# A hybrid attention block: second norm by token halves, stacked low-rank and gate products, modulation sums inside a product tile

## What is computed

```python
mod = silu(c) @ ada_w + ada_b                      # six vectors of 1024
h = rmsnorm(x, norm1_w) * (1 + scale1) + shift1
gq, gk, gv, gr, g_lr, aq, ak, av, ma, mb = split(h @ w_in)     # g_lr has 16 columns
log_a = log_sigmoid(g_lr @ gate_w2 + gate_b) / 16  # [512, 512]
o_gla = rmsnorm(gla_chunked(gq, gk, gv, log_a)) * silu(gr)
y_attn = dilated_attention(aq, ak, av) @ w_attn    # rotary, three groups, 12 heads
x = x + gate1 * ((sigmoid(ma) * (o_gla @ w_gla) + sigmoid(mb) * y_attn) @ w_out)
h2 = rmsnorm(x, norm2_w) * (1 + scale2) + shift2
x = x + gate2 * (conv_ffn_hidden(h2, w_up) @ w_down)           # d_ff 2816
out = rmsnorm(x, final_w)
```

## Time and profile before

| | |
|---|---|
| median of 3 runs | 977.91 us (975.19 to 981.04) |
| the profiled execution as a run | 976.27 us |
| its span, first to last instruction | 974.5 us |
| PE busy | 929.3 us, 95% |
| DVE, ACT, POOL busy | 522.8, 373.1, 95.8 us |
| mean granted clock of PE | 0.969 of 2.4 GHz |
| DMA | 112.68 MB, 116 GB/s mean |

### The profile page before, as it was taken

The page is one execution under the profiler, slowest core; times in us unless marked ns, Lnnn a source line. Parts: engine busy times, 40 slices in busy tenths (PEclk is TensorE's granted clock), DMA queues, the critical chain, the costliest instruction groups (busy, mean ns, idle before and its releaser), DMA issues.

```text
span 974.5 us, 11999 instructions
## 1 busy us (share of the span) xinstructions
PE 929.3 (95%) x4659; PEld 780.5 (80%) x4659; DVE 522.8 (54%) x643; ACT 373.1 (38%) x457; POOL 95.8 (10%) x66
## 2 busy tenths in 40 slices
PE   2689999999999999999999997999999999999996
PEld 2589887779988888888888885888888888888885
DVE  4994775654765546563244436645554556533223
ACT  5362113457543524635222323433433343332225
POOL 4720433000000000000002222000000000000003
PEclk9589999979999999999999998999999999999998
DMA  9925764605253121212232533143334332322302
GB/s 320 362 90 181 212 194 128 212 27 173 91 170 87 44 75 57 87 44 87 86 121 84 184 88 86 49 117 93 86 87 116 99 86 86 125 91 86 123 6 87
DMA packets 114015, 112.68 MB, mean 116 GB/s; under 512 B 4516, under 2 KB 104230, under 8 KB 111671
## 3 DMA queue, kind: packets, MB, share of 16 engines
q1 hardware_dynamic: 113255, 109.96, 35.9%
q10 hardware_dynamic: 720, 2.16, 0.6%
HBM read 104.77 MB, written 4.19 MB: 112 GB/s over the span
## 4 chain that ended last, share of the span: by engine, by line
PE 87%; DVE 6%; DMA 2%; issue 1%; POOL 1%; ACT 1%; SPq 1%; DVEq 0%; POOLq 0%; ACTq 0%
PE bank L1486 25%; PE bank L1488 25%; PE bank L1487 25%; DVE ada_in L959 2%; PE bank L1695 2%; POOL rope L534 1%; PE bank L1877 1%; DMA ada_in<-in_ada_w_dram 1%; PE bank L1641 1%; PE bank L1716 1%; PE bank L1682 1%; PE bank L1578 1%; DVE w_lo L993 1%; DVE h_lo L1414 1%; DMA raw<-in_w_in_dram 1%
## 5 line engine op out<-in xcount | busy, mean ns | idle before, releaser
L1486 PE MATMUL bank<-h_hi,w_hi 128*128 128x512 f32 (+1 forms) x696 | 276.7, 398 | 0.4 <-DVE w_lo L993 0.4
L1488 PE MATMUL bank<-h_hi,w_lo 128*128 128x512 f32 (+1 forms) x696 | 272.4, 391 | 0.0
L1487 PE MATMUL bank<-h_lo,w_hi 128*128 128x512 f32 (+1 forms) x696 | 272.1, 391 | 0.0
L1486 PEld LDWEIGHTS bank<-h_hi,w_hi 128*128 128x128 f32 (+1 forms) x696 | 130.5, 188 | 29.0 <-issue 1.9
L1488 PEld LDWEIGHTS bank<-h_hi,w_lo 128*128 128x128 f32 (+1 forms) x696 | 130.3, 187 | 29.0 <-issue 0.8
L1487 PEld LDWEIGHTS bank<-h_lo,w_hi 128*128 128x128 f32 (+1 forms) x696 | 130.5, 187 | 27.9 <-issue 1.1
L1000 DVE TENSOR_TENSOR w_lo<-raw,w_hi 128x2048 fp32r<-128x2048 f32 x32 | 73.4, 2293 | 88.8 <-ACT w_hi L574 88.8
L993 DVE TENSOR_TENSOR w_lo<-raw,w_hi 128x2048 fp32r<-128x2048 f32 (+3 forms) x48 | 88.2, 1848 | 58.3 <-ACT w_hi L566 58.3
L1440 DVE SCALAR_TENSOR_TENSOR conv<-bank,vecs,conv 128x511 f32<-128x511 f32 x88 | 65.7, 748 | 67.4 <-ACT conv L888 61.9
L566 ACT ACTIVATE w_hi<-raw 128x2048 fp32r<-128x2048 f32 (+2 forms) x45 | 73.4, 1644 | 72.6 <-DMA raw<-in_w_in_dram 64.0
L574 ACT ACTIVATE w_hi<-raw 128x2048 fp32r<-128x2048 f32 x33 | 62.9, 1905 | 69.3 <-PE bank L1488 69.3
(11 more groups left out here) (235 smaller groups left out, 1340.1 us busy)
## 6 DMA issues: line engine op xcount, KB each, us to landing
raw<-in_w_up_dram SPq DMA_DIRECT2D x44, 512.0 KB, 4.6
raw<-in_w_in_dram SPq DMA_DIRECT2D x19, 1024.0 KB, 5.2
raw<-in_ada_w_dram SPq DMA_DIRECT2D x16, 1024.0 KB, 5.5
raw<-in_w_down_dram SPq DMA_DIRECT2D x22, 512.0 KB, 3.9
raw<-in_w_in_dram SPq DMA_DIRECT2D x20, 512.0 KB, 5.2
ada_in<-in_ada_w_dram SPq DMA_DIRECT2D x16, 512.0 KB, 8.9
raw<-in_w_gla_branch_dram SPq DMA_DIRECT2D x4, 1024.0 KB, 5.0
raw<-in_w_out_dram SPq DMA_DIRECT2D x4, 1024.0 KB, 5.3
```

The costliest lines, as they stand in the source:

```text
L1486: pe.matmul(out_ap, wh, xh, start=first, stop=False, skip_group_check=True)
L1487: pe.matmul(out_ap, wh, xl, start=False, stop=False, skip_group_check=True)
L1488: return pe.matmul(out_ap, wl, xh, start=False, stop=last, skip_group_check=True)
```

## The change

- **Second norm.** The last wo unit is computed by token halves: both tiles for tokens 0 to 255 (banks 0, 1), then both for 256 to 511 (banks 6, 7). Squares, sums, inverse root, scale, shift and remainder follow by halves (`wo_part`, `sums`, `scaled`, `second_lo`, `square_half`, `second_hi`). The first up pair takes steps k = 0 to 4 for the first half, then k = 5 to 7 for all tokens, then k = 0 to 4 for the second half (`up_k`). The first two up weights have buffers of their own (`up0_hi` to `up1_lo`), split on ACT and DVE ahead of the norm; POOL's subtraction is gone.
- **Low-rank product.** Its weights are laid out as a stack of 96 columns, three times `hi, lo`. Two matmuls per step k (with `h_hi`, `h_lo`) give six copies, 16 in all instead of 24. ACT writes all 96 rows rounded, DVE replaces rows 32 to 63 with the remainder; the gate weights are rounded and split and stacked by eight DMAs to match, so that one fp32r matmul with 98 rows gives a gate tile. Gate tiles go two at a time to banks 6, 7, after the second gqk tile and after the first gv tile of head 0.
- **Modulation sums.** They are no tile behind a product any more: three of the 16 matmuls follow each step k of the second tile of qk(1,2) and of gr(2), and in `TILES` they now stand ahead of that tile.

```diff
-AFTER_TILE = {(("qk", 1, 2), 1): 0, (("gr", 2, 0), 1): 1}
+WITH_ADA = {(("qk", 1, 2), 1): 0, (("gr", 2, 0), 1): 1}
 for _u in UNITS:
     for _t in range(tiles_of(_u)):
+        if (_u, _t) in WITH_ADA:
+            TILES += [("ada", WITH_ADA[_u, _t])]
         TILES += [(_u, _t)]
-        if (_u, _t) in AFTER_TILE:
-            TILES += [("ada", AFTER_TILE[_u, _t])]
-    if _u == ("gqk", 0, 0):
-        TILES += [("z", b) for b in range(NB)]
...
+                if q == RAW_AT[("w", 5)]:
+                    for row, part in enumerate((g_hi, g_hi, g_hi, g_hi, g_lo, g_lo)):
+                        sp.dma_start(w2s[row * LOWRANK:(row + 1) * LOWRANK, :].bitcast(F32),
+                                     part[w2, :].bitcast(F32)).then_inc(w2s_in, 16)
...
-            pool.tensor_tensor(w_lo[:, 0, :], raw[:, 0, :], w_hi[:, 0, :].bitcast(F32), ALU.subtract).then_inc(raw_used, 1)
...
@@ DVE, qk(1,2)
                         split_lo(n + 1)
+                        ada_tile(0)
                         rotate(GROUPS + g, 1)
-                        ada_tile(0)
...
@@ DVE, after modulate(n) of unit lr
+            free(tile, dve.tensor_tensor(lrT[again, :], src[again, :], lrT[again, :].bitcast(F32), ALU.subtract))
...
@@ DVE, second norm
+            for n in range(len(up_k)):
+                if n == SPLIT_K:
+                    dve.wait_ge(rstd_done, 2)
+                scaled(n)
+                if n == 1:
+                    last_residual(0)
+                if n >= 1:
+                    second_lo(n - 1)
+                if n == 3:
+                    last_residual(1)
...
@@ PE, product
+                elif kind == "lr":
+                    for k in range(KT):
+                        for x_ in (h_hi, h_lo):
+                            last = pe.matmul(dst[0:STACK, :], w_hi[:, slot, k * STACK:(k + 1) * STACK], x_[:, k, :],
...
+                        if ada is not None and k < nk - 1:
+                            ada_part(ada, k)
...
@@ PE, second norm
+            for t in range(2):
+                wo_part(0, t).then_inc(wo_half, 1)
+            wo_part(1, 0, range(KT // 2))
+            sums(0)
+            wo_part(1, 0, range(KT // 2, KT)).then_inc(acc_ready, 1)
+            wo_part(1, 1).then_inc(acc_ready, 1)
```

More of the change, by code:

```diff
@@ L350, in score_blocks, with wo_bank @@
             return [(r * P, P, NB + r) for r in range(DIL)]
+        def wo_bank(half, t):
+            return bank[TILE[("wo", 3, 0), t] % 2] if half == 0 else bank[6 + t]
+        up_w = ((up0_hi[:, :], up0_lo[:, :]), (up1_hi[:, :], up1_lo[:, :]))
+        up_k = ([(k, HALVES[0]) for k in range(SPLIT_K)] + [(k, slice(0, SEQ)) for k in range(SPLIT_K, KT)]
+                + [(k, HALVES[1]) for k in range(SPLIT_K)])
         @block.sync
@@ L871, in _ @@
[L871 to L876, removed]
+            for n in range(SPLIT_K):
+                second_hi(n)
+                if n == 0:
+                    square_half(1, KT - 2)
+                if n == 3:
+                    square_half(1, KT - 1)
@@ L877, in _ @@
+            inverse_root(1, rstd2[:, HALVES[1]], side[3][:, HALVES[1]])
+            for n in range(SPLIT_K, len(up_k)):
+                second_hi(n)
             act.preload_act_table(ACT.Gelu)
@@ L1849, in up_tile, with wo_part @@
-            def up_tile(s, t, k):
-                slot, at = 1 - s, k * UW + t * P
-                w = tuple(v[:, slot, at:at + P] for v in (w_hi, w_lo))
-                return three(bank[2 * s + t][:, :], w, (h_hi[:, k, :], h_lo[:, k, :]), k == 0, k == KT - 1)
+            def wo_part(half, t, ks=range(KT)):
+                n, tok = UNIT[("wo", 3, 0)], HALVES[half]
+                i = TILE[("wo", 3, 0), t]
+                if half == 0:
+                    take(i)
+                    pe.wait_ge(raw_used, RAW_AT[("w", n)] + 1)
+                for k in ks:
+                    at = k * UW + t * P
+                    w = tuple(v[:, n % 2, at:at + P] for v in (w_hi, w_lo))
+                    last = three(wo_bank(half, t)[:, tok], w, (mix_hi[:, k, tok], mix_lo[:, k, tok]), k == 0, k == KT - 1)
+                return last
@@ new lines, in _, with sums @@
+            for t in range(2):
+                wo_part(0, t).then_inc(wo_half, 1)
+            wo_part(1, 0, range(KT // 2))
+            def sums(half):
+                tok = HALVES[half]
+                pe.wait_ge(sum_done, SUMS[1] + KT - 2)
+                pe.matmul(side[2 + half][:, tok], ones[:, :], sq_sum2[:, tok], start=True, stop=False)
+                pe.wait_ge(sq_half if half == 0 else sq_done, 2 if half == 0 else 2 * KT)
+                for m in range(2):
+                    last = pe.matmul(side[2 + half][:, tok], ones[:, :], sq2[:, m, tok], start=False, stop=(m == 1))
+                last.then_inc(ssq_half if half == 0 else ssq_ps, 1)
@@ L1854, in up, with up_tile @@
+            sums(0)
+            wo_part(1, 0, range(KT // 2, KT)).then_inc(acc_ready, 1)
+            wo_part(1, 1).then_inc(acc_ready, 1)
+            def up_tile(s, t, k, w):
+                at = k * UW + t * P
+                w = tuple(v[:, at:at + P] for v in w)
+                return three(bank[2 * (1 - s) + t][:, :], w, (h_hi[:, k, :], h_lo[:, k, :]), k == 0, k == KT - 1)
             def up(a, s, first=False):
@@ L1860, in up @@
                         pe.wait_ge(raw_used, i + (N_RAW + 1))
+                    w = up_w[1] if first else (w_hi[:, 1 - s, :], w_lo[:, 1 - s, :])
                     for k in range(KT):
[L1862 removed]
+                        last = up_tile(s, t, k, w)
                     last.then_inc(ffn_ready, 1)
[L1866 to L1868 removed]
             pe.wait_ge(raw_used, N_RAW + 1)
[L1870 to L1872 removed]
+            for n, (k, tok) in enumerate(up_k):
+                for h_half, ready, halves in ((h_hi, hh2_done, up_w[0]), (h_lo, hl2_done, up_w[0][0:1])):
+                    pe.wait_ge(ready, n + 1)
                     for t in range(2):
@@ L1875, in _ @@
                         for w in halves:
-                            final = k == KT - 1 and h_half is h_lo
-                            last = pe.matmul(bank[t][:, :], w[:, 1, at:at + P], h_half[:, k, :],
-                                             start=(k == 0 and h_half is h_hi and w is w_hi), stop=final,
-                                             skip_group_check=True)
-                        if final:
+                            last = pe.matmul(bank[2 + t][:, tok], w[:, at:at + P], h_half[:, k, tok],
+                                             start=(n == 0 and h_half is h_hi and w is up_w[0][0]),
+                                             stop=(n == len(up_k) - 1 and h_half is h_lo), skip_group_check=True)
+                        if n == len(up_k) - 1 and h_half is h_lo:
                             last.then_inc(ffn_ready, 1)
-            pe.wait_ge(rstd_half, 1)
-            pe.wait_ge(rstd_done, 2)
+                if n == 1:
+                    sums(1)
+            for t in range(2):
+                evacuated(pe, (("wo", 3, 0), t))
             up(0, 1, first=True)
```

268 lines of the change are left out of this document (159 added, 109 removed).

## The result

The changed kernel takes 971.12 us (median of 16 runs, 968.61 to 975.60), the kernel before beside it 977.23 us (16 runs, 975.19 to 981.04): ratio 0.9937, 95% interval 0.9923 to 0.9950. That is 6.1 us less where 13.8 were forecast, and above the range of 957 to 969. The profiled execution took 970.43 us as a run, with a span of 968.5; the one before 976.27, with 974.5.

What follows compares the result with a forecast made beforehand. TensorE, busy 95% of the span, was taken as the bound. First sums and low-rank +1.0, gates -8.5, second norm -6.3 gave -13.8 us, from 976.27 to 962.5 us; range 957 to 969.

Steps and rivals of the forecast that it cites:

- PE's prices: TensorE: a 512-column matmul 0.227 us, a 256-column one 0.119; at the lower clock about 0.42 and 0.211.
- Part 1: First modulation sums and low-rank product: stage +0.6 us, from 19.1 to 19.7; +1.0 carried to the end of the scores.
- The sums keep their 3.5: First modulation sums, now between matmuls of qk(1,2)'s second tile: still cost 3.5 us in all.
- after 3.9 us I expect a fall too, at about 1.6 us, what it costs the low-rank product now: Second tile of qk(1,2): a new 3.9 us bank wait lowers the clock, costing about 1.6 us.
- The +0.4 more that I carried to the end of the scores: Score stage: +0.6 us raised to +1.0 through the score matmuls, after naming weight timing and additions to VectorE's queue.
- Part 2: Gate tiles: four single-pass matmuls save 7.0 us and a clock that stays up saves 1.5; sum -8.5 us.
- Rival B: Half clock returns at the gates after late masks: gates about -6.2, norm -4.8, total 966.3 us; chance 0.18.
- Part 3: Second norm, last output unit to second up pair: -6.3 us from 33.4, range -4 to -7.2.
- Rival C: Second norm: weight loads bind 156 half-width matmuls, 0.069 us more each, +10.8, total 973.3 us; chance 0.04.
- The second set of sums moves from behind a tile into it (...): 0: Second set of modulation sums: same instructions with TensorE full on both sides, charged 0 us.
- D: Slower: the wait at 158 lowers the clock and score-stage waits keep it low: 978.5 to near 987 us; chance 0.03.
- the clock at 0.5 for over 10 us: Granted clock, whole kernel: one of three signs listed that would show the forecast wrong.

Runs made afterwards that it cites:

- Experiment 3: Changed kernel with the bank wait kept but the first modulation sums placed behind the product tile and the attention's transposes: 965.87 us, ratio 0.9887 to the kernel before.
- experiment 2: Changed kernel with the first sums still mixed into the tile but sent to bank 7, so the tile does not wait: 961.09 us, ratio 0.9842 to before.
- experiment 1: Changed kernel with the first modulation sums back in a tile of their own behind the product tile: 963.18 us, ratio 0.9863 to the kernel before.
- experiment 4: Changed kernel with all first sums ahead of the product tile, in the time it waited for its bank: 962.09 us, ratio 0.9848 to the kernel before.
- experiment 6: Kernel before with only the second norm's part of the change: 972.89 us, ratio 0.9936 to the kernel before.
- experiment 7: Kernel before with only the stacked low-rank product and gate products, both sets of sums behind their tiles: 967.30 us, ratio 0.9891 to the kernel before.
- Experiment 8: First sums mixed in through bank 7, plus two waits removed (second sums' bank emptied earlier, reloaded x awaited after the weight split): 958.24 us, ratio 0.9796 to before.
- experiment 5: Changed kernel with its bank wait, first sums entering the tile only from its fifth step, six a step: 967.72 us, ratio 0.9876 to the kernel before.

## Why the prediction was wrong

**What bounds the kernel, and PE's prices: right.** Each us that PE lost or gained in its queue is in the total, and 0.227 and 0.119 us held in every part. At the lower clock a 512-column matmul took 0.43, where 0.42 was worked out.

**Part 1 failed**, at two sentences: "The sums keep their 3.5", and "after 3.9 us I expect a fall too, at about 1.6 us, what it costs the low-rank product now". Place, cause and length of the wait were right (3.46 us, forecast 3.9). The fall was priced from a place where wide matmuls followed it; here one-column sums stood between them, and the lower clock lasted 16 us, 17.0 us for a tile and sums that take 9.4 at the higher one; the forecast had 5.4 + 3.5 + 1.6 = 10.5 for them. So the stage cost +6.7 instead of +0.6. Experiment 3 shows that the wait alone was not it, experiment 2 that the mixing alone was not it. The +0.4 more that I carried to the end of the scores did not come: from first value to scores' end it is 26.6 us in both kernels.

The prediction also took the old low-rank product's half clock as given, and gave it no cause. Experiments 1, 3 and 4 tie it to the block of sums in front of it (the profiles of 6 and 7 have the fall there as well): where that is dissolved and nothing waits, it is gone. Mixing them in is worth 3 us in the stretch (experiment 2 against 1) and 2.1 in the medians; this gain was not in my sum, and the bank wait turned it into a loss.

**Part 2 right**: -8.0 in the profile for -8.5, and the clock stays at 1.00. Rival B did not come in the changed kernel's profile; its mechanism did in experiment 4's.

**Part 3 right**: -6.0 for -6.3; unit finished at 592.75 (592.7 forecast), full steps from 598.11 (598.4), second up pair at 607.02 (606.7); POOL's subtraction is gone. One slip is in its sum: 598.4 + 3 x 1.5 + 5 x 0.9 is 607.4, not 606.7, so the terms as written give -5.6, and the measured value lies between. Rival C falls: 256-column matmuls keep their 0.12 us. By the rule of the Trainium skill that stood beside C, "Perfetto Trace Analysis" (Identifying the Most-Contended Engine), on load instructions as the measure of headroom, they would not have; the measured 0.12 us decides against that reading.

**Left out.** "The second set of sums moves from behind a tile into it (...): 0" was +1.0: DVE empties their bank behind a state step, and PE waits 0.66 us. And the wait for the reloaded x, moved ahead of a weight split, was a line of the diff that I passed over: +0.7 on the way past it. Experiment 8 takes both back.

**The rivals.** D had the mechanism, a wait at 158 that leaves the clock down, and the wrong reason for its length; it decided at 29 us of lower clock, and 16 came. I gave it 0.03 and nothing between it and the forecast's 1.6 us, though the page of the Trainium skill that I named ("TensorE: Matmul & The Clock Gate", HAM oscillation) warns of just such waits. On the fall the trace agrees with it: 0.50 behind 3.46 us of idle time. The failure sign that I wrote down, "the clock at 0.5 for over 10 us", is what came.

In sum: +6.7 - 0.4 - 8.0 + 1.0 + 0.7 - 6.0 = -6.0, against +1.0 - 8.5 - 6.3 = -13.8.

## What to carry to other kernels

When work is moved into a tile of wide matmuls, ask first which bank the tile now takes and who empties it: a slot in an alternating list is part of the change. A short wait is priced by what runs behind it; look for a place in the trace with the same mix of matmuls there, and if there is none, let the range reach from one step to the whole mixed part at the lower clock. Read each moved wait in a diff as a change of its own, even one line long.

## What the hardware showed that I had not expected

- Right after an idle spell of 3.4 us, wide matmuls alone were back at 1.00 within some 6 us (at about 166 after a start at 160.4 in experiment 5; at about 165 after 161.5 in experiment 3); the same matmuls with three sums of one column after each three stayed at 0.50 for 16 us, with PE busy 2.00 of every 2 us.
- A block of 32 one-column passes came with a fall of the clock, within it or up to 1.5 us behind it, in all six profiles that have one at the first site (stretches of 4 us at 0.50 to 0.72; the earlier trace rows for the kernel before). In experiment 4 no idle time stood beside it. At the second site they were in experiments 6 and 7 (0.50 from 342 to 346, 0.53 from 338 to 342), and not in the profile of the kernel before, which has the same instructions there as experiment 6. So one profile does not say what such a block costs; what decides it stays open. The same passes, six after every three wide matmuls, left the clock at 1.00 where no wait had lowered it.
- A one-column pass costs 0.109 us at the higher clock (3.49 us for 32) and 0.21 at the lower (a row of six lasts 1.28), about what a 256-column matmul costs at either.
